# A two-layer fp32 transformer kernel: the last quarter of two output projections moved behind the other three, and the router and last norm reordered to follow the tiles

## The reference

```
first block
  u = rmsnorm(x);  q, kv, k_rope, q_s, k_s, v_s = u @ w_in (and two low-rank projections)
  o_m = softmax attention, 8 heads;  o_s = stick-breaking attention, 8 heads
  h = x + concat(rmsnorm(o_m), rmsnorm(o_s)) @ w_o             # 1024 x 1024: the first out-projection
  logits = rmsnorm(h) @ w_router + b;  4 of 32 experts per token, gates = softmax(top logits)
  h = h + sum over the 4 experts of gate * (clamped SwiGLU of rmsnorm(h) by w_gu) @ w_dn
  h = h + sigmoid(rmsnorm(h) @ w_ple_gate) * (p @ w_ple_proj);  x = rmsnorm(h)
second block
  q, k, v, xr, gr = rmsnorm(x) @ w_in_2
  attn = attention with a bucketed bias;  lru = gated linear recurrence of xr, times gelu(gr)
  mix = concat(attn, lru) @ w_out_2                            # 1024 x 1024: the second out-projection
  x = x + rmsnorm(mix)
  up = causal depthwise conv(rmsnorm(x) @ w_up_2);  x = x + rmsnorm((gelu(g) * u) @ w_down_2)
```

## Time and profile before

| | us |
|---|---|
| median of 3 runs | 1412.57 (1411.61 to 1415.88) |
| the profiled execution | 1414.68 |
| its span | 1412.9 |

### The profile page before, as it was taken

The page is one execution under the profiler, slowest core; times in us unless marked ns, Lnnn a source line. Parts: engine busy times, 40 slices in busy tenths (PEclk is TensorE's granted clock), DMA queues, the critical chain, the costliest instruction groups (busy, mean ns, idle before and its releaser), DMA issues.

```text
span 1412.9 us, 16571 instructions
## 1 busy us (share of the span) xinstructions
PE 1285.8 (91%) x6969; PEld 738.8 (52%) x6969; DVE 489.1 (35%) x735; ACT 400.7 (28%) x641; POOL 59.0 (4%) x115
## 2 busy tenths in 40 slices
PE   7989999999999889988888888888888999899998
PEld 7878543333333333333333333333324898799986
DVE  5795412111211112111121111211113777777765
ACT  5674312100111001110010100101003756755554
POOL 4001000000000000000000000000000510000000
PEclk9998899999999999999999999999999999999999
DMA  9437699999999999999999999999999964355520
GB/s 341 166 125 293 228 383 428 430 425 429 427 426 429 427 429 427 427 428 428 426 428 428 427 428 428 427 427 429 427 427 374 264 222 142 126 182 184 189 103 30
DMA packets 78474, 480.79 MB, mean 340 GB/s; under 512 B 5504, under 2 KB 40475, under 8 KB 53568
## 3 DMA queue, kind: packets, MB, share of 16 engines
q1 hardware_dynamic: 75904, 474.76, 82.9%
q0 software_dynamic: 2496, 4.96, 1.6%
HBM read 478.39 MB, written 1.31 MB: 340 GB/s over the span
## 4 chain that ended last, share of the span: by engine, by line
PE 51%; DMA 40%; DVE 4%; ACT 3%; issue 1%; DVEq 0%; SPq 0%; ACTq 0%
DMA arena<-in_w_dn_dram 38%; PE ps L1937 23%; PE ps L2333 11%; PE ps L2293 10%; DMA ring<-in_w_dn_dram 2%; PE ps L2260 1%; PE ps L2349 1%; DVE W L1224 1%; PE ps L1945 1%; PE ps L2450 1%; ACT arena L898 0%; PE ps L2217 0%; ACT arena L947 0%; PE ps L2304 0%; ACT W L766 0%
## 5 line engine op out<-in xcount | busy, mean ns | idle before, releaser
L2293 PE MATMUL ps<-ring,arena 128*64 128x512 f32 x1392 | 315.3, 597 | 11.8 <-DMA ring<-in_w_gu_dram 11.8
L2293 PEld LDWEIGHTS ps<-ring,arena 128*64 128x64 f32 x1392 | 98.7, 137 | 207.9 <-issue 175.4
L1937 PE MATMUL ps<-X,W 128*128 128x256 f32 x1560 | 189.1, 283 | 2.0 <-DVE W L1230 1.7
L1937 PEld LDWEIGHTS ps<-X,W 128*128 128x128 f32 x1560 | 187.8, 192 | 3.1 <-DVE W L1230 2.2
L1573 DVE TENSOR_SCALAR arena<-ps 128x512 f32<-128x512 f32 x32 | 22.1, 692 | 478.3 <-PE ps L2293 478.3
L1937 PE MATMUL ps<-W,X 128*128 128x512 f32 (+2 forms) x780 | 172.7, 381 | 3.8 <-DVE W L1224 1.9
L1224 DVE TENSOR_TENSOR W<-ring,W 128x2048 fp32r<-128x2048 f32 (+2 forms) x64 | 144.9, 2265 | 75.3 <-ACT W L766 75.3
L2333 PE MATMUL ps<-ring,arena 128*64 128x512 f32 x648 | 145.9, 595 | 22.9 <-DMA ring<-in_w_dn_dram 22.9
L1937 PEld LDWEIGHTS ps<-W,X 128*128 128x128 f32 x780 | 142.1, 188 | 31.8 <-DVE W L1224 4.0
L2293 PE MATMUL ps<-arena 128*64 128x512 f32 x656 | 150.5, 601 | 0.0
L960 ACT ACTIVATE arena<-arena 128x512 f32<-128x512 f32 x32 | 20.2, 631 | 459.3 <-DVE arena L1573 459.3
(11 more groups left out here) (348 smaller groups left out, 996.6 us busy)
## 6 DMA issues: line engine op xcount, KB each, us to landing
ring<-in_w_gu_dram SPq DMA_DIRECT2D x87, 2048.0 KB, 22.4
ring<-in_w_dn_dram SPq DMA_DIRECT2D x40, 2048.0 KB, 24.9
arena<-in_w_gu_dram SPq DMA_DIRECT2D x39, 2048.0 KB, 20.6
arena<-in_w_dn_dram SPq DMA_DIRECT2D x23, 2048.0 KB, 25.6
ring<-in_w_up_dram SPq DMA_DIRECT2D x22, 1024.0 KB, 5.1
ring<-in_w_in_dram SPq DMA_DIRECT2D x15, 1024.0 KB, 12.9
ring<-in_w_down_dram SPq DMA_DIRECT2D x11, 1024.0 KB, 4.9
ring<-in_w_o_dram SPq DMA_DIRECT2D x4, 1024.0 KB, 5.0
```

What stands on the lines that cost most here:

```text
L1937: y = e.matmul(o, l, r, start=start and i == 0, stop=stop and i == 2)
L2293: y = e.matmul(ps[c * 64:c * 64 + 64, use[0], :], xs[:, k, c0:c0 + CAP], w[:, half * D + c * 512:half * D + (c + 1) * 512], start=False, s ...
```

## The change

In both out-projections the last two splits (14 and 15, 32 and 33) are no longer done one after the other for all banks. A new function `rows_part` does one bank's 6 matmuls of a split. The order becomes: 14 for the banks (0,0), (0,1), (1,0); 15 for the same three, which fills them; then, in w_o only, the transposes of tile 0; then 14 and 15 for (1,1). `s_pair` counts split 14 (and 32) after its last bank. The later transposes of h are spread among the logits. `rows_hi` gets a wait for split 14's end.

On VectorE, `scaled(0)` comes after `add_o(0, 1)`, `turned_out(0)` after `add_o(1, 0)`, `scaled(1)` before the loop over the logits. On ScalarE, the copy of tile 1's transposes comes before the square of tile 1. In the mix, tile 0's `square_h` and its root come between the squares of the banks (1,0) and (1,1), with semaphores of their own, and VectorE's reciprocal for it between the gains of these banks.

```diff
@@ -395,10 +395,11 @@
         s_scat = sem("s_scattered")
         act_own, dve_own = sem("s_act_own"), sem("s_dve_own")
         pool = Events(sem("s_pool"), zero=1, ident=1, mzero=2, msk=3, iota=1, one=1, tri=2, i32=1, ez=1, eoh=2, wz=1)
-        squares = Events(sem("s_squares"), attn=2, c=4, sb=2, mla=2, moe=2, ple=2, fin=4, mix=4, ffn=2, end=4)
+        squares = Events(sem("s_squares"), attn=2, c=4, sb=2, mla=2, moe=2, ple=2, fin=4, mix=4, end=4)
         means = Events(sem("s_means"), fin=1)
+        ffn_squares, ffn_roots = (Events(sem("s_ffn_" + n), ffn=2) for n in ("squares", "roots"))
         s_half = Events(sem("s_half_means"), mix=2, end=2)
-        roots = Events(sem("s_roots"), attn=1, c=2, sb=1, mla=1, moe=2, ple=1, fin=2, mix=2, ffn=2, end=2)
+        roots = Events(sem("s_roots"), attn=1, c=2, sb=1, mla=1, moe=2, ple=1, fin=2, mix=2, end=2)
         s_kT = sem("s_k_scaled")
         normed = Events(sem("s_normed"), attn=1, c=1, sb=1, mla=1, gates=1, fin=1, ffn=1)
         x_hi = Events(sem("s_x_hi"), attn=4, c=3, sb=2, mla=2, ple=4, fin=2, fin2=2, lru=4, aT=2, ffn=4)
@@ -555,6 +556,7 @@
             else:
                 n_pair += 1
                 pair_free[s] = (s_pair, n_pair)
+        pair14 = pair_free[14]
         pair_free[14] = BK.filled(U_gath[NE // 4 - 1, 3])
         pair_free[15] = BK.filled(U_y[1][1])
         pair_free.update({56 + j: (s_fused, 2 * j + 2) for j in range(11)})
@@ -778,11 +780,11 @@
                         x = e.activation(hi[:, k + j, :], ps[:, b, j * T:(j + 1) * T], ACT.Copy, scale=gain(k + j))
                     x.then_inc(x_hi.sem, 1)
 
-            def root(n, c, size, last, src=None, bias=epsc):
+            def root(n, c, size, last, src=None, bias=epsc, done=roots.sem):
 
                 e.wait_ge(*last)
                 e.activation(rs[:, c:c + n], ss[:, c:c + n] if src is None else src, ACT.Sqrt, scale=1.0 / size,
-                             bias=bias).then_inc(roots.sem, 1)
+                             bias=bias).then_inc(done, 1)
 
             def half_mean(name, t):
                 e.wait_ge(*squares[name, 2 * t])
@@ -923,14 +925,15 @@
 
             def rows_hi(t, c):
                 e.wait_ge(s_scale, t + 1)
+                e.wait_ge(*pair14)
                 e.activation(uhi[:, t, c].rearrange("q (i p) -> q i p", i=4), by_rows(h[:, t, c]), ACT.Copy,
                              scale=rs[:, t:t + 1]).then_inc(s_uhi, 1)
 
             rows_hi(0, slice(0, 512))
+            e.wait_ge(*BK.filled(U_uT[1][0]))
+            e.activation(uTp[:, 2, :], whole(U_uT[1][0]), ACT.Copy).then_inc(taken[U_uT[1][0][0]], 1)
             e.wait_ge(*h_o(1, 1))
             e.activation(junk_m, h[:, 1, :], ACT.Square, accum_out=ss[:, 1:2]).then_inc(squares.sem, 1)
-            e.wait_ge(*BK.filled(U_uT[1][0]))
-            e.activation(uTp[:, 2, :], whole(U_uT[1][0]), ACT.Copy).then_inc(taken[U_uT[1][0][0]], 1)
             root(1, 1, D, squares["moe", 1])
             rows_hi(0, slice(512, 1024))
             rows_hi(1, slice(0, 512))
@@ -1133,8 +1136,8 @@
             prime(ACT.Sqrt)
             split(34)
 
-            def square_rows(name, t, uses):
-                for n in range(2):
+            def square_rows(name, t, uses, ns=range(2)):
+                for n in ns:
                     e.wait_ge(*BK.filled(uses[t][n]))
                     e.activation(junk[:, t, n * 512:(n + 1) * 512], whole(uses[t][n]), ACT.Square,
                                  accum_out=ss[:, 2 * t + n:2 * t + n + 1]).then_inc(squares.sem, 1)
@@ -1144,18 +1147,19 @@
             def square_h(t):
                 for n in range(2):
                     e.wait_ge(*BK.emptied(U_mix[t][n]))
-                e.activation(u[:, t, :], h[:, t, :], ACT.Square, accum_out=ss[:, t:t + 1]).then_inc(squares.sem, 1)
+                e.activation(u[:, t, :], h[:, t, :], ACT.Square, accum_out=ss[:, t:t + 1]).then_inc(ffn_squares.sem, 1)
 
             square_rows("mix", 0, U_mix)
             root_rows("mix", 0)
-            square_rows("mix", 1, U_mix)
+            square_rows("mix", 1, U_mix, (0,))
+            square_h(0)
+            root(1, 2, D, ffn_squares["ffn", 0], ss[:, 0:1], done=ffn_roots.sem)
+            square_rows("mix", 1, U_mix, (1,))
             root_rows("mix", 1)
-            square_h(0)
-            root(1, 2, D, squares["ffn", 0], ss[:, 0:1])
             e.wait_ge(s_r0, 1)
             e.activation(u[:, 0, :], h[:, 0, :], ACT.Copy, scale=rs[:, 2:3]).then_inc(s_u0, 1)
             square_h(1)
-            root(1, 3, D, squares["ffn", 1], ss[:, 1:2])
+            root(1, 3, D, ffn_squares["ffn", 1], ss[:, 1:2], done=ffn_roots.sem)
 
 
             for t in range(2):
@@ -1509,19 +1513,18 @@
 
             add_o(0, 0)
             add_o(0, 1)
+            scaled(0)
             add_o(1, 0)
+            turned_out(0)
             add_o(1, 1)
 
 
-            scaled(0)
-            turned_out(0)
+            rows_lo(0, slice(0, 512), 1)
             turned_out(1)
-            rows_lo(0, slice(0, 512), 1)
+            scaled(1)
             e.wait_ge(s_brt, 16)
             e.wait_ge(*pool["i32", 0])
             for t in range(2):
-                if t:
-                    scaled(1)
                 e.wait_ge(*BK.filled(U_l[t]))
                 e.scalar_tensor_tensor(out=lg[:, t, :], in0=whole(U_l[t], NE), scalar=rs[:, t:t + 1], in1=brt, op0=ALU.mult,
                                        op1=ALU.add).then_inc(taken[U_l[t][0]], 1)
@@ -1857,16 +1860,19 @@
             over_root("mix", 0, 0, 1)
             for n in range(2):
                 add_rows(0, n, U_mix)
-            gained_rows("mix", 1, U_mix, gmix)
+            gained("mix", 1, 0, U_mix, gmix)
+            e.wait_ge(*ffn_roots["ffn", 0])
+            e.reciprocal(rs[:, 2:3], rs[:, 2:3]).then_inc(s_r0, 1)
+            gained("mix", 1, 1, U_mix, gmix)
             over_root("mix", 1, 1, 1)
-            add_rows(1, 0, U_mix)
-            e.wait_ge(*roots["ffn", 0])
-            e.reciprocal(rs[:, 2:3], rs[:, 2:3]).then_inc(s_r0, 1)
-            add_rows(1, 1, U_mix)
+            for n in range(2):
+                add_rows(1, n, U_mix)
             hi, lo = halved(34)
             e.wait_ge(s_hi, 35)
             e.tensor_tensor(lo[:, 0:4], loads[SPL[34]][0][:, 0:4], hi[:, 0:4].bitcast(F32), ALU.subtract)
-            over_root("ffn", 1, 3, 1)
+            e.wait_ge(*ffn_roots["ffn", 1])
+            step(e.reciprocal(rs[:, 3:4], rs[:, 3:4]))
+            e.wait_ge(*own.now())
             e.tensor_scalar(u[:, 1, :], h[:, 1, :], rs[:, 3:4], None, ALU.mult).then_inc(normed.sem, 1)
             e.tensor_tensor(lo[:, 4:8], loads[SPL[34]][0][:, 4:8], hi[:, 4:8].bitcast(F32), ALU.subtract).then_inc(s_lo, 1)
 
@@ -1965,6 +1971,19 @@
                                 (hi[:, kk0 + i, c], lo[:, kk0 + i, c]), k == k_first, k == k_last, True)
                         if k == k_last:
                             y.then_inc(full[use[0]], 1)
+                return y
+
+            def rows_part(s, ks, t, n, uses, x_ready, last):
+
+                hi, lo = halved(s)
+                e.wait_ge(*lo_done(s))
+                use, c = uses[t][n], slice(n * 512, (n + 1) * 512)
+                for i, k in enumerate(ks):
+                    e.wait_ge(*x_ready(k))
+                    y = mm3(whole(use), [z[:, k, t * P:(t + 1) * P] for z in xin], (hi[:, i, c], lo[:, i, c]), False,
+                            last and k == ks[-1], True)
+                if last:
+                    y.then_inc(full[use[0]], 1)
                 return y
 
             def rows_first(s, ks, uses, x_hi_ready, x_ready, part_free):
@@ -2207,8 +2226,24 @@
             for i in range(2):
                 turned(U_mT[i], mlh, 2 * i, 2)
             rows_in(13, (6, 7), 0, U_o, xin, 4, 3, 512, 1024, sT_ready).then_inc(s_pair, 1)
-            rows_in(14, (0, 1), 0, U_o, xin, 4, 3, 512, 1024, mT_ready).then_inc(s_pair, 1)
-            rows_in(15, (2, 3), 0, U_o, xin, 4, 3, 512, 1024, mT_ready, by_tile=True)
+            for t, n in ((0, 0), (0, 1), (1, 0)):
+                rows_part(14, (0, 1), t, n, U_o, mT_ready, False)
+            for t, n in ((0, 0), (0, 1), (1, 0)):
+                rows_part(15, (2, 3), t, n, U_o, mT_ready, True)
+
+            def turned_rows(t, half):
+                x = U_uT[t][half]
+                claim(x)
+                e.wait_ge(*h_o(t, half))
+                for q in range(4):
+                    k = 4 * half + q
+                    y = e.transpose(ps[:, x[0], q * P:(q + 1) * P], h[:, t, k * P:(k + 1) * P], ident[:, :])
+                y.then_inc(full[x[0]], 1)
+
+            turned_rows(0, 0)
+            turned_rows(0, 1)
+            rows_part(14, (0, 1), 1, 1, U_o, mT_ready, False).then_inc(s_pair, 1)
+            rows_part(15, (2, 3), 1, 1, U_o, mT_ready, True)
 
             def bias(x):
                 e.wait_ge(s_Ex, x + 1)
@@ -2218,20 +2253,14 @@
                              start=True, stop=False)
 
 
```

(20 more changed lines are left out.)

## The result

| | before | changed |
|---|---|---|
| median of 7 runs, us | 1412.65 (1411.61 to 1416.02) | 1418.66 (1417.55 to 1420.61) |
| ratio to before, 95% interval | | 1.0043 (1.0033 to 1.0052) |
| profiled execution's span | 1412.9 | 1416.9 |

A forecast was written before the change was run, and what follows sets the result against it. Bound by stretches: expert weight transfers (DMA) after the router, TensorE alone after the mix, so delays arrive in full. 5.62 + 1.1 + 0 = +6.7 on the profiled 1414.68 gave 1421.4, as median 1419.3; range 1415.1 to 1422.7.

The forecast's parts named there:

- The held split: Mix: ScalarE's split 34 waits for split 32's last quarter, starts 4.53 us late, and holds the squares behind it.
- The order of the norms: End of the mix: all of tile 0's work now comes behind the last matmul, losing 1.09 us.
- The whole distance: Mix, split 31's first matmul to the first copy into X: 5.62 us longer, from 4.53 and 1.09.
- The stalls for a low part: TensorE waits for the low part of split 33 in the mix, 0.37 us, and of split 15 at the router, 0.26.
- The router: Router: a wait of 0.40 us removed less a new stall of 0.26, gain 0.14, taken as 0.
- The covers: Router: VectorE's wait for the root (1.7 us), rows_hi's wait (0.3) and POOL's later cast (1.2) stay off the path.
- One sign of being wrong: Router: the forecast is wrong if SP's restart at 159.57 moves by over a microsecond.
- one of being right: Router: the second tile's logits end within 0.3 us of where they did before.
- rival 3: Worse: low clock beyond 3 us in the mix, or falling earlier in the router (+1.9); 1421 to 1424; chance 0.12.
- The clock term: First w_up matmuls after the mix start at the low clock for some 3 us: +1.1, bounds 0 to 1.6.
- rival 1: Split held, but clock back before the dense matmuls and one drop less in the router: 1415.1 to 1417.2; chance 0.17.
- Rival 2: Mix: the squares are not held by split 34, so the kernel is faster, 1409.3 at best; chance 0.04.

The follow-up runs named there:

- e4: The changed kernel with ScalarE's split 34 moved behind the squares and tile 0's scaling; median 1414.46 us, ratio to the kernel before 1.0006.
- e5: The changed kernel, but in the mix TensorE goes bank by bank as before, only the norms' order being new; ratio to the kernel before 0.9998.
- e3: The changed kernel, but in the mix ScalarE and VectorE keep the old order, only TensorE's being new; ratio to the kernel before 1.0027.
- e1: The kernel before with the change at w_o and the router alone, mix as before; median 1414.26 us, ratio 0.9996.
- e2: The kernel before with the change in the mix alone, w_o and router as before; median 1418.95 us, ratio 1.0038.
- e8: The kernel before with two added matmuls, their result unwanted, in each of three places at the router; ratio 1.0001.
- e11: The kernel before with one added matmul, its result unwanted, in each of three places at the router; median 1412.61 us, ratio 0.9989.
- e7: The kernel before with 7 added matmuls, their result unwanted, behind split 33 in the mix; ratio 1.0002.
- e12: The kernel before with one added matmul at each of three router places and 4 in the mix; median 1410.60 us, ratio 0.9981.

## Why the prediction was right

**The held split** was the step that carried it. Forecast: 4.53 us late; measured 4.64 for split 34 (15.84 against 11.20) and 4.63 for the first square (17.66 against 13.03). e4 shows that it is the cause, since only the place of split 34 on ScalarE differs there, and e5, since the hold goes with TensorE's order. The Trainium skill (TensorE: Matmul & The Clock Gate, Architectural detail) states that ScalarE is strictly first in, first out, and the trace agrees: 6.64 us idle ahead of split 34 with a full bank behind it in the program.

**The order of the norms** was forecast at 1.09, as what the distance has beyond the start of split 34. By the same subtraction it measured 0.95 (27.33 less 15.84, against 21.74 less 11.20); on top of e3 it is 1.28, and alone in e5 0.98. The whole distance was forecast at +5.62 and came at +5.59. The reason that I gave, that all of tile 0's work now comes behind the last matmul, is too narrow: in e5 nothing is held, and the square of h in front of the last bank's square costs the same 0.98.

**The stalls for a low part** were forecast at 0.37 in the mix and 0.26 at the router. From start to start, at 0.231 us a matmul, they were 0.36 and 0.28. The one in the mix is a part of the 4.64: three quarters of split 33 (4.15), this stall, and 0.1 more.

**The router** was taken at 0. The router stretch is 28.21 us on average over seven traces with the new router (27.85 to 28.36), and 28.53 over four with the old (28.04, 28.12, 28.49 and the 29.46 of the trace read beforehand). Its gain is nothing that the ratio of e1, 0.9996 (0.9987 to 1.0004), can tell from zero. The covers held: VectorE's wait for the root, the new wait in rows_hi and POOL's later cast are not on the chain. But I had added up TensorE's waits only. The logits that lost theirs left the chain, and VectorE took their place; so it is in the traces of e1, e3, e4 and e5 too, while in e2, with the old router, the second tile's logits are still on it.

One sign of being wrong came, and one of being right did not: SP's restart moved by 2.21 us (159.57 to 157.36), and the second tile's logits ended 1.1 us early where 0.3 was allowed, the 0.8 ahead of split 14 taken off. Neither is the change's doing as far as the runs show: e2, with the old router, ends those logits at 146.14 and restarts the queue at 157.14. The signs were set tighter than executions differ. Two readings in the forecast were off without touching its sum. A w_dn transfer stands in the chain for 21 of the 32 experts, from 424.40 on, and not for every one. And if all 16 logits ran at the low level they would take twice 1.87, so 3.7 us and not 4.7: rival 3's price is +0.9, and the high end of the range would be 1421.7.

**The clock term, +1.1, was mis-sized for the medians.** In the pair of profiled executions it was 1.33, so the mechanism was there: the dense matmuls began at 0.50 and stayed there for 4.0 us (3 were forecast), from 1221.60 to about 1225.6. But I took the one trace of before as what the kernel before does. In four traces with its mix unchanged the first bank is read 9.12, 10.92 (e1), 11.25 (e8) and 10.01 (e11) us behind the first copy, 10.3 on average; in the changed kernel and e2 it is 10.45 and 10.38. The kernel before seems to start w_up at the low clock more often than not, so on medians the term is about 0.1, an estimate from these six traces. The upper bound of 1.6 was too low besides: e1 and e8 lie 1.80 and 2.13 us above the trace of before. It went by 0.15 us for a gather matmul at the high level, where 16 in 2.14 us (e11) make 0.134. With 0.1 the sum is 5.6 + 0.1 + 0 = +5.7, and 6.0 was measured, inside the interval of 4.7 to 7.3 us. The sum of the forecast, +6.7, is inside it too, but by a term that should not have been there; that 1419.3 came so near to 1418.66 is in that part luck.

**Rivals.** The kinder clock (rival 1) came in its half at the router and not in the mix: the clock fell about 147, a little behind the second tile's logits, and the router stretch was 1.4 us shorter than in the trace of before, but e2 with the old router shows the same 28.04, so it was the execution and not the change. Rival 2 is excluded by the 6.64 us of idle time. Of rival 3 the low clock lasted longer than the 3 us, but the time stayed below its 1421.

## What to carry to other kernels

Before matmuls are reordered so that a result is ready sooner, list every event that they give, and who waits for it: a buffer of two halves gives its release with the *last* use of a half, and moving one quarter of that use to the end moves the next fill too. If that fill stands, in an engine that works in order, ahead of the work that was to profit, the profit is gone and more. Count the other engines too: what one engine no longer waits for is gained only if none of them takes its place on the chain, as VectorE did at the router. And where an engine's clock differs from one execution to the next, one trace is no base for a term; take the same stretch from several.

## What was not expected of the hardware

- TensorE's granted clock falls at the router and in the mix's gap in the kernel before as well, and where it falls and rises differs between executions of the same instructions: the first 48 w_up matmuls took 6.47 us from the first to the end of the last in the trace of before and 8.27 in that of e1.
- It also falls without a long gap. In the trace of before it fell at about 146.1, and since 124.57 TensorE had not been idle for more than the 0.40 us ahead of 145.20; transposes and 128x32 logits were what it last did. In e2, with the same router, it stood up through them, and these 16 took 1.94 us instead of 2.80.
- Matmuls that compute nothing wanted can make a kernel faster. One in each of three gaps (1.10 us each in the trace of e11) went with a clock of 2.4 GHz through the router, a gather of 2.14 us instead of 3.75, and a stretch of 27.1 instead of 28.5; with four more in the mix the kernel gained 0.19% (0.10 to 0.28). It is not sure to work: with seven in the mix (e7) and with four (e12) the clock fell there all the same.
- A 128x512 fp32 matmul by the 128x128 identity takes 0.87 us (16 in 13.89, two records each). The experts' matmuls of the same width, with 64 weight columns, take 0.23 to 0.25 us per record (16 records in 3.68 us in the changed kernel, and in 3.97, begun at the low level); I had sized an added matmul at twice that. They go in pairs to the two halves of a bank's partitions; whether the pairs overlap was not tried by itself.
